# Expert layers: a slot for 32 tokens and four experts with column groups, and the sample's slots behind the first tile

## The reference

```python
def peer(h, w_q, sub_keys, u_tab, v_tab):
    q = (xf @ w_q).reshape(n, H_P, 2, D_HALF)
    s = jnp.einsum('nhcd,hckd->nhck', q, sub_keys).astype(jnp.float32)
    s_top, i_top = lax.top_k(s, TOPK)
    cand = (s_top[:, :, 0, :, None] + s_top[:, :, 1, None, :]).reshape(n, H_P, TOPK * TOPK)
    c_top, c_idx = lax.top_k(cand, TOPK)
    ...
    ids = i1 * N_KEYS + i2
    gates = jax.nn.softmax(c_top, axis=-1).astype(h.dtype)
    ...
        act = jax.nn.gelu(jnp.einsum('td,thkd->thk', xb, u_tab[ib]), approximate=False) * gb
        return jnp.einsum('thk,thkd->td', act, v_tab[ib])
```

## Time and profile before

| | |
|---|---|
| timed runs, median of 3 | 3477.43 us |
| span of the profiled execution | 3501.1 us |
| PE busy, of the span | 2983.7 us, 85% |
| VectorE / ScalarE / POOL busy | 62% / 41% / 37% |
| mean granted TensorE clock | 0.965 of 2.4 GHz |
| first gather of the first and second layer | 322.7 / 2172.7 us |
| HBM read | 1188 MB |

### The profile page before, as it was taken

One profiled execution on the slowest core, in us unless ns is written; L12 is line 12 of the kernel. 1 busy time (PEld: TensorE's weight loads), 2 busy tenths in 40 slices (PEclk: granted clock), 3 DMA queues, 4 the chain that ended last, 5 costly groups with the idle time before them and its releaser, 6 DMA issues. The chain is left out here.

```text
span 3501.1 us, 34014 instructions
## 1 busy us (share of the span) xinstructions
PE 2983.7 (85%) x10561; PEld 1480.5 (42%) x10561; DVE 2185.4 (62%) x5266; ACT 1438.0 (41%) x4182; POOL 1301.9 (37%) x1112
## 2 busy tenths in 40 slices
PE   8987888888889888887999886888888888888886
PEld 7653333433334433333554764434333434433332
DVE  4874667666667766664362334666766676766765
ACT  3122445444444544443351222444444444544444
POOL 0211444444544444452001010445444454444442
PEclk9988999999999999999999897999999999999999
DMA  4015999999999999998203345999999999999998
GB/s 163 29 52 228 421 421 414 421 421 415 420 398 421 418 421 421 421 419 350 81 1 162 134 165 220 421 421 414 421 421 421 415 408 421 409 421 421 421 419 355
DMA packets 178372, 1194.53 MB, mean 341 GB/s; under 512 B 22320, under 2 KB 28240, under 8 KB 38150
## 3 DMA queue, kind: packets, MB, share of 16 engines
q0 software_dynamic: 154368, 1128.34, 77.8%
q1 hardware_dynamic: 22525, 63.11, 4.8%
q10 hardware_dynamic: 1296, 0.90, 0.1%
HBM read 1188.29 MB, written 4.46 MB: 341 GB/s over the span
## 5 line engine op out<-in xcount | busy, mean ns | idle before, releaser
L1581 PE MATMUL p_acc<-p_rows,p_diag 128*128 128x512 f32 (+1 forms) x4160 | 1973.0, 616 | 412.8 <-ACT p_diag L1184 411.0
L1414 DVE CUSTOM_DVE_ANT_0 p_rows<-p_rows,p_x_n 128x1024 f32<-128x1024 f32 x1024 | 1243.7, 1223 | 790.5 <-DMA p_rows<-in_peer_uv,p_ids 788.4
L1096 POOL DMA_INDIRECT p_rows<-in_peer_uv,p_ids x1024 | 1217.0, 1188 | 1384.6 <-PE p_acc L1581 1281.6
L1581 PEld LDWEIGHTS p_acc<-p_rows,p_diag 128*128 128x128 f32 (+1 forms) x4160 | 752.9, 192 | 1508.5 <-ACT p_diag L1184 790.8
L1178 ACT ACTIVATE p_acts<-p_dots 128x1 f32<-128x1 f32 x1040 | 208.3, 200 | 871.8 <-DVE p_dots L1414 870.4
L1184 ACT ACTIVATE p_diag<-ident,p_gated 128x128 f32<-128x128 f32 x1024 | 410.9, 401 | 33.6
L1180 ACT ACTIVATE p_gated<-p_acts,p_gates 128x1 f32<-128x1 f32 x1024 | 301.6, 295 | 33.2
L1531 PE MATMUL p_q_bank<-p_w_q,p_xT 128*128 128x256 f32 x1024 | 234.9, 383 | 2.2 <-ACT p_xT L1127 2.2
L1531 PEld LDWEIGHTS p_q_bank<-p_w_q,p_xT 128*128 128x128 f32 x1024 | 196.1, 192 | 55.5 <-issue 28.5
L1150 ACT COPY p_q_rows<-p_q_bank 128x256 f32<-128x256 f32 x68 | 25.2, 370 | 347.7 <-PE p_q_bank L1531 347.7
L1623 POOL DMA_INDIRECT smp_past<-in_cache_rows,smp_row_ids x32 | 30.0, 937 | 361.1 <-PE c_ps L2096 227.4
(11 more groups left out here) (402 smaller groups left out, 2483.0 us busy)
## 6 DMA issues: line engine op xcount, KB each, us to landing
p_w_q<-in_w_q_heads SPq DMA_DIRECT2D x16, 1024.0 KB, 12.2
p_rows<-in_peer_uv,p_ids POOLq DMA_INDIRECT x1024
a_w_in<-in_ab_w_in SPq DMA_DIRECT2D x6, 1024.0 KB
a_w_in<-in_ab_w_out SPq DMA_DIRECT2D x1, 4096.0 KB
c_arena<-in_c_w_out SPq DMA_DIRECT2D x1, 4096.0 KB, 12.7
smp_past<-in_c_w_out SPq DMA_DIRECT2D x1, 4096.0 KB
a_w_in<-in_ab_w_in SPq DMA_DIRECT2D x4, 1008.0 KB, 21.3
smp_past<-in_w_qx SPq DMA_DIRECT2D x1, 3072.0 KB, 18.6
```

What stands on the lines that cost most here:

```text
L1096: nc.gpsimd.indirect_dma_start(out=rows[:, slot % RING, :], out_offset=None, in_=w[f"peer_uv{layer}"], in_offset=bass.IndirectOffsetOnAxis ...
L1414: nc.vector.tensor_tensor_reduce(rows[:, k % RING, 0:D_MODEL], rows[:, k % RING, 0:D_MODEL], x, 1.0, 0.0, ALU.mult, ALU.add, dots[:, slot ...
L1581: last = nc.tensor.matmul(acc[done % 2][0:n, at], diag[:, slot // GROUP % 4, j, 0:n], rows[:, (slot + j) % RING, D_MODEL + 512 * b:D_MODEL ...
```

## The change

A slot is no longer one expert of 128 tokens. It is now four experts of 32 tokens: partition 32e + i holds token i of quad q (32 tokens) and its expert of number e, e + 4, e + 8 or e + 12, so that head n still has 16 slots, four to each quad. Each gather still brings 128 rows. For this,

- x is kept four times: x_rep[:, q] holds the 32 tokens of quad q on all four partition groups. TensorE makes it with a 32x128 matrix (spread_x) through the bank that also turns x, ScalarE copies it out (x_rep_out), four times per tile.
- ids and gates are turned the same way: routing writes pick, TensorE spreads it with 16 small products (spread_picks), VectorE copies ids and gates, and only then picked releases POOL. The early lookup of eight ids is gone.
- The weights are a 128x32 matrix (fold times weight) in place of the diagonal. The product sums over the four experts, and the 1024 columns go as four parts of 256 to four column groups, whose results stand on four partition groups of PSUM.
- Adding to x takes 16 additions of 32x256 per tile in two halves: quads 0 and 1 at pair 5 of the tile's last head, quads 2 and 3 behind pair 1 of the next.
- The sample's chain is at heads 0 to 4, its eight slots between tile 0 and tile 1, with the same column groups.
- The last gain takes the buffer of the layer's gain, late in the layer.

```diff
-SMP_AT = NW - H_P
+SMP_AT = H_P
+QUAD, QUADS, PARTS = 32, 4, 4
+D_PART = D_MODEL // PARTS
 TILE_ENDS = tuple(H_P * t + H_P - AHEAD - 1 for t in range(NT - 1))
 END_ORDER = (0, 1, 2, NT, 3)
-SMP_NORM, SMP_FIRST, SMP_SECOND, SMP_ROUTE = 16, 18, 19, 20
+SMP_NORM, SMP_FIRST, SMP_SECOND, SMP_ROUTE = 0, 2, 3, 4
...
-        x_n = sb("x_n", [128, 2, D_MODEL])
+        quads = sb("quads", [128, 128])
+        x_n = sb("x_n", [128, D_MODEL])
+        x_rep = sb("x_rep", [128, QUADS, D_MODEL])
...
-        diag = sb("diag", [128, 4, GROUP, 128])
+        weights = sb("weights", [128, 4, GROUP, QUAD])
...
-        acc = [psum("acc0", [128, D_MODEL]), psum("acc1", [128, D_MODEL])]
+        acc = psum("acc", [128, QUADS, D_PART])
+        acc_smp = psum("acc_smp", [128, 512])
+        pick_bank = psum("pick_bank", [128, 512])
...
+        by_quad = pick_bank[:, 0:2 * TOPK].rearrange("p (q c j) -> p q c j", q=QUADS, c=2)
...
-                if n == 0:
-                    pool.wait_ge(routed_early, 1)
-                else:
-                    pool.wait_ge(routed, route_no(n) + 1)
+                pool.wait_ge(picked, n + 1)
                 for k in range(TOPK):
-                    if n == 0 and k == 8:
-                        pool.wait_ge(routed, 1)
                     gather(first_slot(n) + k, ids[:, n % (AHEAD + 1), k:k + 1])
...
+            def x_rep_out(t, q):
+
+                act.wait_ge(turn_ps, rep_turn(t, q) + 1)
+                if t:
+                    act.wait_ge(dotted, first_slot(H_P * t - 1) + QUADS * (q + 1))
+                nc.scalar.copy(x_rep[:, q, :], turn[:, :]).then_inc(turn_used, 1)
...
-                    nc.scalar.mul(diag[:, i % 4, j, 0:n], unit[:], gated[:, i % 4, j:j + 1]).then_inc(diag_ready, 1)
+                    nc.scalar.mul(weights[:, i % 4, j, 0:n], unit, gated[:, i % 4, j:j + 1]).then_inc(weights_ready, 1)
...
+            x_rep_out(0, 0)
+            x_rep_out(0, 1)
             q_out(1)
             qT_out(1, qT[:])
+            x_rep_out(0, 2)
             exps(0)
             s_out(1)
+            x_rep_out(0, 3)
             exps(1)
...
-                act.wait_ge(gates_ready, route_no(n) + 1)
+                act.wait_ge(picked, n + 1)
+                grown = n // H_P + 1 if n % H_P == H_P - 1 and n < NW - 1 else 0
...
+                if grown:
+                    x_rep_out(grown, 0)
...
+            def spread_picks(m):
+
+                dve.wait_ge(pick_ps, m + 1)
+                nc.vector.tensor_copy(ids[:, m % (AHEAD + 1), :].rearrange("p (q j) -> p q j", q=QUADS), by_quad[:, :, 0, :])
+                nc.vector.tensor_copy(gates[:, m % (AHEAD + 1), :].rearrange("p (q j) -> p q j", q=QUADS), by_quad[:, :, 1, :]).then_inc(picked, 1)
...
-            def add_to_x(done, t):
-
-                n = rows_of(t)
-                dve.wait_ge(rows_used, (128, 256, 384, 392, 520)[done])
-                nc.vector.tensor_tensor(x_sb[0:n, t, :], x_sb[0:n, t, :], acc[done % 2][0:n, :], ALU.add).then_inc(acc_used, 1)
+            def add_to_x(t, bank):
+
+                for q in (2 * bank, 2 * bank + 1):
+                    dve.wait_ge(rows_used, first_slot(H_P * t + H_P - 1) + QUADS * (2 * bank + 2))
+                    for c in range(PARTS):
+                        at = x_sb[quad(q), t, part(c)]
+                        last = nc.vector.tensor_tensor(at, at, acc[quad(c), q, :], ALU.add)
+                last.then_inc(acc_used, 1)
...
-                if m == 0:
-                    pairs(m, ids[:, m, :])
-                    lookup_second(ids[:, m, :])
-                else:
-                    pairs(m)
-                    lookup(m, ids[:, m, :])
-                softmax(m, gates[:, m, :])
+                pairs(m)
+                lookup(m, pick[:, 0, :], m)
+                softmax(m, pick[:, 1, :])
+                spread_picks(m)
...
                 for g in range(GROUPS):
                     slot = first_slot(n) + GROUP * g
-                    dot(slot, x, (2 * g - 12, 2 * g - 11) if out and n == NW - 1 and g >= 6 else ())
+                    if n % H_P == 0 and g % 2 == 0:
+                        dve.wait_ge(turn_used, rep_turn(t, g // 2) + 1)
+                    dot(slot, x_rep[:, g // 2, :], (2 * g - 12, 2 * g - 11) if out and n == NW - 1 and g >= 6 else ())
                     if g == 0 and n in TILE_ENDS:
                         normalise(t + 1)
                     if g == 0 and n == SMP_NORM:
                         smp_normalise()
-                    if g == 1 and n in (H_P, 2 * H_P):
-                        add_to_x(t - 1, t - 1)
+                    if g == 1 and n % H_P == 0 and n and n != SMP_AT:
+                        add_to_x(t - 1, 1)
+                    if g == 2 and 0 < n < NW - 1:
+                        spread_picks(n + 1)
+                    if g == 5 and n % H_P == H_P - 1:
+                        add_to_x(t, 0)
...
+            def spread_x(t, q):
+
+                if t == 0 and q == 0:
+                    pe.wait_ge(small_in, 80)
+                pe.wait_ge(turn_used, rep_turn(t, q))
+                for b in range(2):
+                    at = slice(512 * b, 512 * b + 512)
+                    last = nc.tensor.matmul(turn[:, at], quads[quad(q), :], x_n[quad(q), at], start=True, stop=True)
+                last.then_inc(turn_ps, 1)
...
+            def spread_picks(m):
+
+                pe.wait_ge(routed, route_no(m) + 1)
+                pe.wait_ge(gates_ready, route_no(m) + 1)
+                if m:
+                    pe.wait_ge(picked, m)
+                for q in range(QUADS):
+                    for e in range(4):
+                        last = nc.tensor.matmul(by_quad[quad(e), q], ident[:, quad(q)], pick[:, :, e:TOPK:4], start=True, stop=True)
+                last.then_inc(pick_ps, 1)
+
+            def experts(slot, dst, n, first, end):
+
                 for j in range(GROUP):
-                    pe.wait_ge(diag_ready, slot + j + 1)
-                    for b in range(2):
-                        at = slice(512 * b, 512 * b + 512)
-                        last = nc.tensor.matmul(acc[done % 2][0:n, at], diag[:, slot // GROUP % 4, j, 0:n], rows[:, (slot + j) % RING, D_MODEL + 512 * b:D_MODEL + 512 * b + 512],
+                    pe.wait_ge(weights_ready, slot + j + 1)
+                    for c in range(PARTS):
+                        at = D_MODEL + D_PART * c
+                        last = nc.tensor.matmul(dst[QUAD * c:QUAD * c + n], weights[:, slot // GROUP % 4, j, 0:n], rows[:, (slot + j) % RING, at:at + D_PART],
                                                 start=(first and j == 0), stop=(end and j == GROUP - 1))
                     last.then_inc(rows_used, 1)
...
+                spread_x(0, 2 * m)
+                spread_x(0, 2 * m + 1)
+            spread_picks(0)
+            spread_picks(1)
...
-                    experts(first_slot(n) + GROUP * g, done, 128, n % H_P == 0 and g == 0, n % H_P == H_P - 1 and g == GROUPS - 1)
+                    q = g // 2
+                    if t and h == 0 and g % 4 == 0:
+                        pe.wait_ge(acc_used, 2 * (t - 1) + g // 4 + 1)
+                    experts(first_slot(n) + GROUP * g, acc[:, q, :], QUAD, h == 0 and g % 4 == 0, h == H_P - 1 and g % 4 == 3)
+                    if g == 0 and 0 < n < NW - 1:
+                        spread_picks(n + 1)
...
+                    if g % 2 and h == H_P - 1 and t < NT - 1:
+                        spread_x(t + 1, q)
```

173 lines of the change are left out of this document (80 added, 93 removed).

## The result

The changed kernel takes 3519.2 us (median of 4 runs, 3517.4 to 3521.2) where the kernel before takes 3477.2 (3475.9 to 3477.6): a ratio of 1.0118, 95% interval 1.0104 to 1.0133, 42 us slower. I had forecast 3489 with a range up to 3503.

What follows compares the result with a forecast made beforehand. The prediction took DMA gathers at 421 GB/s to bound the expert layers. Starts +19.3, steady heads -10 and ends +2.7 made +12 us on the 3477.4 median: 3489, range 3478 to 3503.

Steps and rivals of the forecast that it cites:

- What bounds it, and the ceiling: Expert layers' plateaus: DMA gathers bound at 421 GB/s; a faster TensorE can give back at most 18 us.
- The slot: Each slot's product: eight records, four column groups side by side, 0.46 us at full clock, twice that at half.
- The start, 19.3 us: Both layer starts: first gather 11.2 us late, DMA idle 9.6 us per layer, 19.3 for both.
- my 33.9: Layer 1's start: first gather expected some 33.9 us behind the block's first DMA.
- The steady heads, -10 us: Heads after the start: 18 us of stalls regained less 8 at tile starts, gain 10, bounds 4 and 18.
- a limit of 11.8: Head starts: free if the first slot is released within about 11.8 us of the last dot before it.
- The ends, +2.7 (0.5 and 2.2): Both layer ends: shorter last product, eight adds for one; 0.5 and 2.2 us, sum 2.7, bounds 0 and 5.
- The bytes: Transfers in the expert layers: the prediction had no term for added bytes.
- The rivals: Start gap only 3481 (0.20); column groups serial 3503 (0.06); VectorE becomes brake 3540 (0.05); transfer rate rises 3468 (0.08).
- The sample's move at nothing: Sample's chain moved to heads 0 to 4, its slots behind tile 0: hidden by the same waits, worth nothing.
- The base: Whole kernel: absolute terms added to the timed median 3477.4, which lies 23.7 us below the profiled span 3501.1.

Runs made afterwards that it cites:

- best4: Changed kernel: adds in twos and fours, late spreads in tile's first head, third start spread before second ids turn, ScalarE weighing before query copy; ratio 1.0023 to before.
- warm3: Changed kernel with three unused 128x256 matmuls behind every slot's product, outside the sample's slots and the head behind them; 18 us slower than the changed kernel.

## Why the prediction was wrong

The places were right: a gap at each layer's start, dips at tile starts alone, a small price at the ends. Two terms were mis-sized, both to the same side, and one was left at nothing.

- **What bounds it, and the ceiling.** Right: before loses 16.8 us in its heads by the windows, where I had 18. Away from the tile starts after loses about 1.5 (26.6 less some 25 in the six dips), so 15 us came back there. But the dips took the steady stretches to 415 and 416, not to 420.
- **The slot.** Right: a slot's 8 records take 0.64 us with the drain at full clock and 1.08 at half, so the column groups run side by side; nothing of it shows. PE was busy 63% of the span, where I had said under 50%.
- **The start, 19.3 us: measured 29.9.** The step that failed is the one that took durations of the full clock for a stretch full of waits. From the scores on, the second handover was 1.4 us longer (spread 3.15) and the queries 2.3 (5.89 for 3.62). The fourth spread stood ahead of the ids' turn, which I had left beside it (1.6). The small matmuls gave 0.9 back. That is 4.4 of the 5.4 us by which the first gather missed my 33.9; the rest lies ahead of the scores, where the first queries took 6.34 us and not the 5.20 of the earlier trace rows (6.47 in the second trace of before).
- **The steady heads, -10 us: measured +9.8 by the windows, some 6 to the last data.** The step that failed is the last head of a tile. I added VectorE's eight adds (3 us) to the way from the last dot to the first release, made that 14 us, and held it against a limit of 11.8 read off. The 14 came out, 14.5, but by luck. The adds stand ahead of the last dot, not behind it, so they are not in the 14.5. What fills it is the last pair's product (2.5 us to its end, for 1.8), the spread (3.8, for 2 to 3) and the queries (5.98, for 5.2), at the lower clock. And the adds, by making the last dot late, cut the limit: counted from its end, 9.2 us here and not 11.8, since the queue held only 7.6 us of data at its last issue. 14.5 less 9.2 is the stall of 5.3, where I had 2 to 3. I had also put one such stall aside for head 8, which loses 1.6 to 2.4.
- **The ends, +2.7 (0.5 and 2.2): measured +4.3 (1.3 and 3.0)** from the last data on, inside the bounds. The eight adds cost 2.2 us over the one add, and the last product, at the lower clock, gave back 0.9 and not 1.3. In the second layer 1.7 more lies ahead of the last dot, as I had it.
- **The bytes, at nothing.** An estimated 2.3 us of transfers, mostly instructions, had no term.
- **The rivals.** None came. The sample's move at nothing was right by two experiments.
- **The base.** Adding the terms to the timed median, not to the span, was right, but the 24 us between them were not those of a profile being taken: a second one did not have them.

best4 can be closed the same way: the last add of its layers comes 4.1 and 3.8 us later than before's, 7.9 against 7.8 timed. 3.5 of it is behind the last data (1.3 and 2.2), an estimated 2.3 the bytes, and some 2 more idle time of the queue over both layers, with 6.2 more at the starts and most of it regained behind them. Open is what a full clock would give at a layer's start: no run had it there.

## What to carry to other kernels

A margin counted from an engine's last work holds only while that engine comes as early as in the old trace. Count what the queue still holds at its last issue (issued less moved) against the way from there to the next one, and sort every added piece by which of the two it changes: here adds ahead of the last dot shrank the first, spreads and queries behind it stretched the second. Where an engine is relieved, price its chains of handovers also at the lower clock. And what a layout change adds at a boundary (spreads, small adds) can be placed where it is first read: the same instructions, moved, gave 34 of the 42 us back.

## What the runs showed of the hardware

TensorE's granted clock was 0.50 from 2165 to 2171 in the layer's start of after, behind waits of 0.5, 0.6 and 1.1 us, where I had seen it fall behind one of 2.8. Later it stood at 0.50 from 1630 to 1650, where each slot's product took 1.08 us. In warm3, with work that nothing waits for, it was 0.98 over the steady stretch, and the kernel 18 us slower.

The instruction queue moved 2.20 MB in after and 1.38 in before, on the same DMA engines and inside the plateaus.

The same kernel before took 3477 in most sets and 3504.7 in one, with the difference in one stage that no edit touched. A comparison across sets would have been wrong by two thirds of the effect.
